# A two-layer encoder trunk on one core: two gathered rows per routing round, eight per full round of the last stage, fused one-hot products, 76 blocks ahead of the last stage

## The reference

```
def peer_ffn(xn, wq, sub_keys, expert_u, expert_v):
...
        q = (x @ wq).reshape(C, PEER_HEADS, 2, PEER_HALF)
        s = jnp.einsum('chpk,hpnk->chpn', q, sub_keys).astype(jnp.float32)
        top_s, top_i = lax.top_k(s, K)
        cand = top_s[:, :, 0, :, None] + top_s[:, :, 1, None, :]
        best_s, best_j = lax.top_k(cand.reshape(C, PEER_HEADS, K * K), K)
        i1 = jnp.take_along_axis(top_i[:, :, 0], best_j // K, axis=-1)
        i2 = jnp.take_along_axis(top_i[:, :, 1], best_j % K, axis=-1)
        e = i1 * N_KEYS + i2
        g = jax.nn.softmax(best_s, axis=-1).astype(x.dtype)
        u = jnp.take(expert_u, e, axis=0)
        h = jax.nn.gelu(jnp.einsum('cd,chkd->chk', x, u))
        v = jnp.take(expert_v, e, axis=0)
        return jnp.einsum('chk,chkd->cd', g * h, v)
```

## Time and profile before

| | us |
|---|---|
| median of three runs | 3505.8 |
| the profiled execution's own time | 3508.56 |
| its span, first to last instruction | 3506.7 |
| TensorE matmuls busy | 3253.6 (93%) |
| VectorE busy | 2486.3 (71%) |
| ScalarE busy | 1245.7 (36%) |
| GpSimd busy | 1157.5 (33%) |
| data moved | 763.87 MB, mean 218 GB/s |

### The profile page before, as it was taken

The page is one execution under the profiler, slowest core; times in us unless marked ns, Lnnn a source line. Parts: engine busy times, 40 slices in busy tenths (PEclk is TensorE's granted clock), DMA queues, the critical chain, the costliest instruction groups (busy, mean ns, idle before and its releaser), DMA issues.

```text
span 3506.7 us, 55600 instructions
## 1 busy us (share of the span) xinstructions
PE 3253.6 (93%) x17714; PEld 2868.3 (82%) x17714; DVE 2486.3 (71%) x4700; ACT 1245.7 (36%) x2013; POOL 1157.5 (33%) x647
## 2 busy tenths in 40 slices
PE   7999999788789999999999999996886999999999
PEld 6787799677678888888877877996776888888887
DVE  4554599999687767676645445998996877767675
ACT  4333332333233333333334333333332333333332
POOL 3443344101233333333134433441103333333331
PEclk9999999889989999999989999998898999999999
DMA  3211344577888888888621113445778998898885
GB/s 120 68 48 57 111 134 130 202 261 274 295 314 317 302 309 299 303 296 305 211 97 67 54 60 109 133 136 204 272 257 311 324 318 296 306 305 305 298 301 204
DMA packets 235870, 763.87 MB, mean 218 GB/s; under 512 B 19056, under 2 KB 117488, under 8 KB 200688
## 3 DMA queue, kind: packets, MB, share of 16 engines
q1 hardware_dynamic: 198896, 494.09, 40.4%
q0 software_dynamic: 36864, 268.45, 22.3%
HBM read 684.87 MB, written 77.59 MB: 217 GB/s over the span
## 4 chain that ended last, share of the span: by engine, by line
PE 60%; DVE 18%; DVEq 10%; issue 7%; DMA 3%; POOL 1%; ACT 1%; SPq 0%; POOLq 0%; ACTq 0%
PE PS L418 18%; PE PS L420 18%; PE PS L419 18%; DVEq L1354 3%; DVEq L1358 2%; DVE OB L1356 2%; PE PS L585 2%; DVE OE L1353 1%; DVE EQS L1277 1%; PE PS L692 1%; DVEq L1325 1%; DVE I L1223 1%; DVE I L1230 1%; DVE SW L1224 1%; POOL RL L1431 1%
## 5 line engine op out<-in xcount | busy, mean ns | idle before, releaser
L1431 POOL TENSOR_TENSOR RL<-RAW,RH 128x1024 fp32r<-128x1024 f32 x320 | 797.3, 2501 | 782.5 <-ACT RH L764 782.0
L418 PE MATMUL PS<-XH,RH 128*128 128x384 f32 (+1 forms) x2720 | 993.1, 365 | 23.1 <-ACT GEL L951 23.1
L420 PE MATMUL PS<-XH,RL 128*128 128x384 f32 (+1 forms) x2720 | 963.3, 354 | 0.0
L419 PE MATMUL PS<-XL,RH 128*128 128x384 f32 (+1 forms) x2720 | 961.5, 354 | 0.0
L1465 POOL DMA_INDIRECT ROWS<-in_peer_rows,LIST x256 | 292.1, 1141 | 1428.8 <-DVE X L1326 1392.6
L418 PE MATMUL PS<-VHI,WHI 128*128 128x512 f32 x1536 | 601.3, 392 | 37.6 <-DVE WLO L1388 37.6
L419 PE MATMUL PS<-VLO,WHI 128*128 128x512 f32 x1536 | 600.9, 391 | 0.0
L420 PE MATMUL PS<-VHI,WLO 128*128 128x512 f32 x1536 | 600.8, 391 | 0.0
L418 PEld LDWEIGHTS PS<-XH,RH 128*128 128x128 f32 x2720 | 522.5, 192 | 51.6 <-issue 24.4
L1385 DVE TENSOR_TENSOR VLO<-VRAW,VHI 128x1024 fp32r<-128x1024 f32 x256 | 319.8, 1249 | 338.0 <-ACT VHI L959 338.0
L419 PEld LDWEIGHTS PS<-XL,RH 128*128 128x128 f32 x2720 | 522.1, 192 | 27.6
(11 more groups left out here) (231 smaller groups left out, 3396.3 us busy)
## 6 DMA issues: line engine op xcount, KB each, us to landing
RAW<-in_peer_u SPq DMA_DIRECT2D x256, 512.0 KB, 5.1
VRAW<-in_peer_v SPq DMA_DIRECT2D x256, 512.0 KB, 5.8
RAW<-in_stream SPq DMA_DIRECT2D x128, 512.0 KB, 3.3
route_dram<-STAGE SPq DMA_DIRECT2D x16, 3072.0 KB, 12.7
GC<-route_dram SPq DMA_DIRECT2D x64, 768.0 KB, 8.8
gelu_dram<-GS SPq DMA_DIRECT2D x128, 192.0 KB, 3.7
GB<-gelu_dram SPq DMA_DIRECT2D x32, 768.0 KB, 9.8
ROWS<-in_peer_rows,LIST POOLq DMA_INDIRECT x256, 7.3
```

Of the source, the lines that this page charges most:

```text
L418: pe.matmul(acc, sh, mh, start=first, stop=False)
L419: pe.matmul(acc, sh, ml, start=False, stop=False)
L420: return pe.matmul(acc, sl, mh, start=False, stop=last)
L1431: pool.tensor_tensor(RL[:, k % 4, :], RAW[:, k % 2, :], RH[:, k % 4, :].bitcast(F32), ALU.subtract).then_inc(S.low_part, 1)
```

## The change

Constants: `FILLED` goes from 64 to 76, `FIRST` from 30 to 32. Of the 44 blocks between, 40 lie in the eight routing rounds (five a round in place of four), the other 4 behind them (before: 32 and 2). The last stage keeps its 16 rounds and 128 positions, but only 13 of them (`FULL`) have blocks of their own; the last three read all eight gelus from DRAM. Slots: 2 in a routing round in place of 3, 2 in place of 6 between the stages, 8 in each of the 13 full rounds in place of 6 (the first had 8 already), 2 in each of the last three. The order of the positions changes with that, and `peer_u` is laid out on the host in that order.

Routing on VectorE: the two one-hot tables are one instruction of 2048 elements (`OAE`), the three products one of 3072. The gate product moves to ScalarE, as a second activation behind the gelu that waits for the first. The loops over rounds are written out. SyncE's order between the stages is new.

```
-FILLED = 64
-FIRST = 30
+FILLED = 76
+FIRST = 32
+FULL = (NK - FILLED) // 4
...
-AT_Q = (0, 1, 2, 4, 5, 6)
-LOW_AT = (1, 2, 4, 5)
+EVERY = tuple(range(8))
+AT_Q = (EVERY,) + (EVERY[:8],) * (FULL - 1) + ((1, 5), (1, 5), (1, 5))
+LOW_AT = (0, 1, 2, 4, 5)
+R_FILLS = 40
+THREE = 3 * len(AT_Q[1])
+STEPS = tuple(range(40 * s // 12, 40 * (s + 1) // 12) for s in range(12))
...
-S_ROUTE, S_TURN, S_FIRST, S_POS = 24, 6, 8, 6
+S_ROUTE, S_TURN = 16, 2
...
+                sp.wait_ge(S.routing_stored0, count(l, "routing_stored0", 64))
+                apart(sp)
+                position(0, 0)
+                position(0, 1)
...
+                load_next(0)
+                load_next(1)
+                store_gelu(FILLED - 4, 0)
+                load_next(2)
+                store_gelu(FILLED - 3, 1)
+                sp.wait_ge(S.routing_stored1, count(l, "routing_stored1", 64))
...
                 load_filled(0)
+                store_gelu(FILLED - 2, 2)
+                load_next(3)
+                load_new(0)
...
+                            for j in range(5):
+                                ks = [s % KD for s in STEPS[g] if s // KD == j]
+                                if ks:
+                                    f = FIRST + 5 * r + j
+                                    fill(20 * i + f, J_U + 20 * i + f, f % 4, 6 + f % 2, ks)
...
-                    act.activation(ACTED[:, c:c + 1], DOT[:, c:c + 1], ACT.Gelu_apprx_tanh).then_inc(S.scored, 1)
+                    act.activation(ACTED[:, c:c + 1], DOT[:, c:c + 1], ACT.Gelu_apprx_tanh).then_inc(S.acted, 1)
+                    act.wait_ge(S.acted, count(l, "acted", k + 1))
+                    act.activation(SHARE[:, c:c + 1], ACTED[:, c:c + 1], ACT.Copy,
+                                   scale=GATES[:, bass.ds(k, 1)]).then_inc(S.scored, 1)
...
-                    dve.tensor_tensor(SHARE[:, c:c + 1], ACTED[:, c:c + 1], GATES[:, bass.ds(k, 1)], ALU.mult)
-                    dve.drain()
...
-                        dve.tensor_tensor(tokens(OA[:, slot]), numbers, of_tokens(0), ALU.is_equal)
-                        dve.tensor_tensor(tokens(OE[:]), numbers, of_tokens(1), ALU.is_equal)
+                        dve.tensor_tensor(tokens(OAE[:, slot]), numbers, of_tokens(KEYNO, 2), ALU.is_equal)
                         dve.drain()
-                        for p in range(3):
-                            m = dve.tensor_tensor(tokens(OB[:, slot, p]), tokens(OE[:]), of_tokens(2 + p), ALU.mult)
+                        m = dve.tensor_tensor(OB[:, slot].rearrange("p r t (i d) -> p r (t i) d", d=2),
+                                              OAE[:, slot, 1].rearrange("p t (i d) -> p (t i) d", d=2).unsqueeze(1).to_broadcast(
+                                                  [P, 3, 8 * P // 2, 2]), of_tokens(PARTS, 3), ALU.mult)
```

More of the change, by code:

```diff
@@ L334, in _ @@
                     store_gelu(FIRST + k - 4, (FIRST + k) % 4)
[L335 to L359, removed]
+                with sp.Fori(0, 2) as i:
+                    for r in range(4):
+                        for k in range(5):
+                            f = FIRST + 4 + 20 * i + 5 * r + k
+                            slot = (FIRST + 5 * r + k) % 4
+                            load_experts(J_U + f, f, slot % 2)
+                            store_gelu(f - 4, slot)
+                        store_routing(4 * i + r, r % 2)
                 def load_filled(it):
@@ L733, in outputs_and_hidden, with outputs @@
                     hidden(it + 1, 3)
+                def outputs(it, pairs=4):
+                    for pair in range(pairs):
+                        output(it, pair)
                 for m in range(4):
@@ L739, in _ @@
                 outputs_and_hidden(0, True)
-                with pe.Fori(1, 15) as it:
+                with pe.Fori(1, FULL - 1) as it:
                     outputs_and_hidden(it)
-                for pair in range(3):
-                    output(15, pair)
+                for it in range(FULL - 1, 15):
+                    outputs(it)
+                outputs(15, 3)
                 output(15, 3, last=True)
@@ L961, in position, with positions @@
                     act.activation(WHI[:, q % 4, :], WF[:, q % 2, :], ACT.Copy).then_inc(S.weighted_high, 1)
-                def positions(it, k, at_q, ahead):
+                def positions(n, it, j, now, next1, next2):
+                    at_q, k = AT_Q[n], first_slot(n)
                     for q in range(8):
@@ L1470, in low_of @@
                     low(0, n)
[L1472 to L1473 removed]
+                for n in range(J_U + FIRST - 4, J_U + FIRST):
+                    low_of(n)
                 low_of(J_U + FIRST)
[L1475 removed]
                 pool.wait_ge(S.experts_listed, count(l, "experts_listed", 1))
@@ L1545, in laid_out @@
             edge[g, 1, c] = 2 * h / min(PAD - c + h, 2 * h)
+    filled = [8 * (f // 4) + f % 4 if f < 64 else 8 * (FULL + f // 4 - 16) + 4 + f % 4 for f in range(FILLED)]
+    order = filled + [8 * (c // 4) + 4 + c % 4 for c in range(NK - FILLED)]
     inv = (10000.0 ** (-np.arange(0, ROPE, 2, dtype=np.float64) / ROPE)).astype(f)
```

262 lines of the change are left out of this document (139 added, 123 removed).

## The result

The changed kernel takes 3390.21 us (median of 4 runs, 3385.91 to 3392.29) against 3505.39 (3502.85 to 3505.9) for the kernel before, run beside it: a ratio of **0.9671, 95% interval 0.9654 to 0.9688**. It is faster by 115 us. 3365 was forecast, so the sum was 25 us too favourable. The profiled execution's span is 3390.5 us, with TensorE busy for 95% of it.

What follows compares the result with a forecast made beforehand. TensorE, busy 93%, was taken as the bound, with VectorE bounding routing. Per layer -21.5 - 10 - 40 + 1.5 = -70 us, two layers 141 off 3505.8, gave 3365 us; range 3315 to 3455.

Steps and rivals of the forecast that it cites:

- Ahead of routing: Before routing: two more blocks (8.3 us) fit into 14.8 us of waiting; their low parts cost 1.5 us a layer.
- Routing, -21.5: Eight routing rounds at 31.3 us, with 2 us held back for the first round's clock: 21.5 us less a layer.
- Between, -10: From last routing group to first output: near 49 us in place of 58.7, 10 us less a layer.
- block 81 ... can be loaded only when block 79's low part is made, near 36: Between the stages: block 81's load starts near 36 us, leading to the first output near 49.
- Last stage, -40: Last stage: 12 full rounds at 49.8 us, a thirteenth at 39.5, three at 34.5; 741 in place of 781.1 us.
- eight positions on two buffers: Each of the last three rounds: 34.5 us, with 3.1 MB of gates and gelus between.
- I take 49.8: Last stage: each of 12 full rounds takes 49.8 us, with TensorE at 49.4 and the round with holds at 48.5.
- I am wrong if a full round is over 51 us: Last-stage sign of error: then see whether `VHI` waits for `VRAW`, `dot` for `ROWS`, or `WF` for GpSimd.
- The gate product: Off VectorE: 0.24 us less a slot; eight (1.9 us) taken off a 51.2 us last-stage round, giving 48.5 with 0.8 of waiting.
- The fused instructions: Rival, in routing: they lose their rate, a round takes 16 us more, the kernel 3625 us; 4%.
- The transfers bound the full rounds: Rival, last stage: 17.0 MB a round at 323 GB/s takes 52.8 us, the kernel 3470 us; 25%.
- TensorE is the only bound: Rival, all stages: routing -26, between -17, last stage -48, -90 us a layer, the kernel 3326 us; 15%.

Runs made afterwards that it cites:

- e_rawfirst: The changed kernel with U blocks 76 and 77 loaded ahead of the first two V blocks of the last stage: 3395.15 us.
- e_ordpos: The changed kernel with the load moves of e_rawfirst and e_order, and position 0 on ScalarE ahead of the high parts of blocks 80 and 81: 3352.24 us.
- e_order: The changed kernel with the two U blocks of each half round of the last stage loaded one position later, same bytes: 3364.76 us.
- e_half: The changed kernel with the last stage's gathers reading only the u half of each row, which changes the routed sum: 3354.04 us.
- e_dvelow: The changed kernel with the low parts of the full rounds' U blocks made on VectorE instead of GpSimd: 3440.43 us.
- e_ordgate: The kernel of e_order with the product of score and gate back on VectorE: 3407.42 us.
- e_latehi: The changed kernel with high parts of blocks 80, 81 made behind position 1 and V loads of positions 2, 3 ahead of blocks 82, 83: 3395.25 us.

## Why the prediction came out as it did

**Ahead of routing, +1.5 a layer.** +1.3 in layer 0. The wait for the choice fell from 14.8 to 6.3 us a layer, where two blocks of 4.17 in it would leave 6.5, so the cover is as forecast:

```profile
PE PS L707 <- DVE GW L1339: 12.6, 2, 6.3
```

In layer 1 it is -5.0, but the same stretch takes 632 to 638 us in the profiles of the experiments, none of which touches it. These 5 us are not explained, and that they bring the sum nearer to the forecast is luck.

**Routing, -21.5.** -20.7 and -20.4. Rounds are 30.1 to 33.8 us, 31.4 in the mean of seven (31.3 forecast); the fourth, at 33.8 and 32.8 (over 33 was named as a sign of being wrong), is the one that holds the turn of TensorE's loop. The profile gives `OAE` 1.22 and `OB` 1.76 us (1.23 and 1.77 forecast) and a clock of 0.99:

```profile
L1400 DVE TENSOR_TENSOR OB<-OAE,PARTS 128x3072 bf16<-128x3072 bf16 x96 | 168.8, 1758 | 7.2
L1398 DVE TENSOR_TENSOR OAE<-IOTAB,KEYNO 128x2048 bf16<-128x2048 bf16 x96 | 117.2, 1221 | 7.2 <-PE PS L720 4.8 <-issue 2.3
```

The closeness of the total is in part luck. 274.1 less 8 x 31.3 is 23.7, not 23.5. And the stage ends with its eighth round's last group, which took 30.0 us before and takes 29.4 now: seven rounds saved 20 us and the eighth 0.6, where eight savings of 2.9 had been counted. The 2 us that were taken off for the clock of the first round made up for most of that.

**Between, -10.** -3.4 and -1.4: the step that failed is "block 81 ... can be loaded only when block 79's low part is made, near 36", and the low part of block 79 starts at 40.0 and is made at 42.4. The rows of after that answer to the earlier trace rows:

```profile
904.58 6.94 SPq L285 DMA_DIRECT2D RAW<-in_peer_u  x2
...
920.49 1.06 ACT L800 ACTIVATE RH<-RAW 128x1024 fp32r<-128x1024 f32 x1 [11.41 <-DMA RAW<-in_peer_u]
...
929.36 0.35 SPq L285 DMA_DIRECT2D RAW<-in_peer_u  x1
...
936.53 1.06 ACT L800 ACTIVATE RH<-RAW 128x1024 fp32r<-128x1024 f32 x1 [5.62 <-DMA RAW<-in_peer_u]
...
937.67 2.37 POOL L1475 TENSOR_TENSOR RL<-RAW,RH 128x1024 fp32r<-128x1024 f32 x1 [4.29 <-ACT RH L800]
...
945.50 2.59 DVE L1434 TENSOR_TENSOR VLO<-VRAW,VHI 128x1024 fp32r<-128x1024 f32 x1 [10.17 <-ACT VHI L1001]
```

The last routing group ends at 897.7. Block 76 had been put near 20, with 5 to 7 us of waiting, and its high part is made at 22.8, with 11.4 us of waiting. Each load after it carries that on, and block 79's waits behind gates and gelus once more. The first output is at 55.6, not 49. e_rawfirst shows the first part (4 to 5 us of it stand behind two V blocks that nobody needs yet), e_ordpos the last one (ScalarE's order, 3 us more).

**Last stage, -40.** -31.7 and -34.7. The four last rounds take 135.8 and 137.1 us where 143 had been forecast, 6 to 7 better: "eight positions on two buffers" cost less than I took (98.8 us for the last three, 103.5 forecast, and 37.0 and 38.3 for the thirteenth, 39.5 forecast). The full rounds are the term that was mis-sized, 598 forecast and 613.6 and 607.6 measured. "I take 49.8" assumed that a round which is just long enough on both engines stays even. In layer 0, at 51.1, the prediction's own sign for this term came true ("I am wrong if a full round is over 51 us"), and of the three waits that it told to look at it was the first, `VHI` for `VRAW`. The hold that was forecast did come (`WF` held 5.7 us, as in the earlier trace rows), and it costs nothing in e_order and e_half. What I lacked was the burst. I had weighed the mean demand against the mean rate, 345 against 342 GB/s. The mean fits: e_order runs at 345 with no gap. But a gelu load and two U blocks stand ahead of a V block with a single buffer's lead, and it then takes 11 us, not 6. The full rounds were 18 and 12 us over those of e_order, and that one move took all of it away.

In layer 0 the terms add up so, measured less forecast: ahead of routing -0.2, routing +0.8, between +6.6, full rounds +15.6, last four rounds -7.2, in all some 15.6 us. The mis-sizing of the full rounds is larger than it looks in the total, since the last four rounds gave half of it back. The mechanism of the full rounds, and not only their number, was incomplete.

**The gate product** was priced at 0.24 us a slot of VectorE's time, and mostly as part of the 48.5 us round. In the last stage 19 and 20 us a layer hang on it, of the 32 and 35 won there. That can be read only once VectorE's round is added up with its holds, as above: by that sum it lies within some 1 us of TensorE's.

**The rivals.** The fused instructions kept their rate. "The transfers bound the full rounds" (52.8 us) was half right: transfers did lengthen them, to 51, but by their order and not by their volume at 323 GB/s. "TensorE is the only bound" came true for the full rounds in e_order, at 49.6, though its 3326 us was not reached: 3352 is the best (e_ordpos), with 250 us in routing where that rival had 244, 48 between where it had 42, and 137 to 138 in the four last rounds where it had 133.

The Trainium skill ("DMA: Bandwidth & Descriptors", Specifications) gives some 358 GB/s for a core. The highest mean over a stretch of 600 us here is 345 (e_order), so by that rule the queue was near its end but not at it, and the runs agree. Over short stretches the rate was above that figure: 362 GB/s in 50 us and 395 in 20 us of e_order (2619 to 2669, 1407 to 1427). The exclusion of VectorE and GpSimd that the Trainium skill states ("SBUF — State Buffer", the section on the memory's two sides) showed in each full round of the changed kernel, `WF` at 5.67 us in place of 0.56, and not in e_dvelow, where GpSimd had no low parts there. What it costs depends on what else is late: nothing in e_order.

## What to carry to other kernels

A load that is issued just in time, because its buffer comes free late, should have nothing large ahead of it in the queue that could as well stand behind it: one such move was worth 25 us here, with the same bytes, and a mean rate that fits says nothing about it. When an engine shows 86% busy, add up one round of it with the times in which its instructions are held: here that came to TensorE's own round, and 0.24 us a slot, eight times a round, was worth 43 us (e_ordgate). And what is won at the head of a stage must be followed into its first round, which took one such gain back whole and another in part; in e_latehi it was a gather, behind low parts in a third engine's queue, that took it back.

## What the runs showed of the hardware

**A stall at the turn of a long loop.** With the gate product or the low parts on VectorE, the body of its loop in the last stage is longer, and VectorE then idles at each turn (every three rounds) for 4.8 to 6.9 us, "issue", which no semaphore explains. In the changed kernel and in e_order its longest such gap is 0.8 us. The timeline of e_ordgate at two turns, then instruction transfers (packets, MB, share) in 960 to 1560 of e_order and of e_ordgate:

```profile
1302.09 0.56 DVE L1432 TENSOR_TENSOR WF<-GB,GC 128x384 f32<-128x384 f32 x1 [6.54 <-issue]
...
1454.14 0.72 DVE L1432 TENSOR_TENSOR WF<-GB,GC 128x384 f32<-128x384 f32 x1 [6.16 <-issue]
```

```profile
q14 instruction: 9, 0.07, 0.0%
```

```profile
q14 instruction: 25, 0.20, 0.1%
```

The transfers of instructions grow from 9 to 25 with it, and in each of the three idle stretches of e_ordgate's layer 0 (VectorE has nothing in 1143.4 to 1149.5, 1295.6 to 1302.0 and 1448.1 to 1454.1) one or two of them fall. So it seems that code is loaded again at each turn. That this load is what VectorE waits for is read from these together and was not tried alone; which queue serves which engine no row tells. In e_ordgate it costs little by itself (the halves at a turn are 0.6 us longer than the others), since TensorE is ahead by more.
